# Norm statistics held by tokens, one number each, and spread over the features by TensorE

## What is computed

```python
def rms_norm(x, g):                       # mix0, ctx, ffn0, mix1, ffn1, fin, mix2, mlp2
    y = x * lax.rsqrt(jnp.mean(x * x, axis=-1, keepdims=True) + EPS)
    return y * g

def gated_deltanet(qkv, z, ...):          # 8 heads of 128
    q, k, v = jnp.split(jax.nn.silu(causal_depthwise_conv(qkv, conv_w)), 3, axis=-1)
    q, k = l2norm(q), l2norm(k)           # x * rsqrt(sum(x * x) + EPS), by head
    o = chunk_gated_delta_rule(q, k, v, g, beta)
    o = rmsnorm(o, out_norm) * jax.nn.silu(z)

def nsa_mixer(q, ..., k_s, ..., k_w, ...):   # heads of 64
    q = rmsnorm(q, q_norm) * (d ** -0.5)     # and rmsnorm of k_s and k_w
```

## Time and profile before

| what | value |
|---|---|
| median of 3 runs | 1294.68 us (1292.54 to 1296.09) |
| the profiled execution: its own time | 1292.29 us |
| its span, first to last instruction | 1290.5 us |
| mean clock granted to TensorE, share of full speed | 0.948 |
| PE busy | 1157.9 us, 90% of the span, 9,918 records |
| PEld busy | 1090.2 us, 84% |
| DVE busy | 899.5 us, 70% |
| ACT busy | 603.6 us, 47% |
| DVE `RECIPROCAL` on 128x512, 10 of them | 33.5 us |
| DVE `RECIPROCAL` on 128x256, 8 of them | 14.1 us |

### The profile page before, as it was taken

One profiled execution on the slowest core, in us unless ns is written; L12 is line 12 of the kernel. 1 busy time (PEld: TensorE's weight loads), 2 busy tenths in 40 slices (PEclk: granted clock), 3 DMA queues, 4 the chain that ended last, 5 costly groups with the idle time before them and its releaser, 6 DMA issues.

```text
span 1290.5 us, 23296 instructions
## 1 busy us (share of the span) xinstructions
PE 1157.9 (90%) x9918; PEld 1090.2 (84%) x9918; DVE 899.5 (70%) x1561; ACT 603.6 (47%) x1085; POOL 55.3 (4%) x70
## 2 busy tenths in 40 slices
PE   5878589999987999997988788778999999799999
PEld 1776479999987999996988676667998999799999
DVE  4956858988886666545668687878864975777443
ACT  2435535445445444543544556574323455555432
POOL 0000010000011000001000000001420001000000
PEclk9989789999998999999788898989999999899999
DMA  9741638888872575531344222112211555755520
GB/s 390 305 189 45 241 142 324 336 341 334 309 312 88 194 281 222 197 107 66 106 163 158 99 82 81 67 66 76 90 35 67 196 189 171 266 195 195 202 79 13
DMA packets 32360, 226.35 MB, mean 175 GB/s; under 512 B 3584, under 2 KB 4736, under 8 KB 5120
## 3 DMA queue, kind: packets, MB, share of 16 engines
q1 hardware_dynamic: 30528, 221.20, 46.3%
q10 hardware_dynamic: 1728, 3.67, 0.8%
HBM read 223.80 MB, written 1.05 MB: 174 GB/s over the span
## 4 chain that ended last, share of the span: by engine, by line
PE 63%; DVE 24%; ACT 9%; DMA 2%; issue 2%; POOL 0%; SPq 0%; DVEq 0%; ACTq 0%; POOLq 0%
PE bank L525 19%; PE bank L527 18%; PE bank L526 18%; DVE sb_wlo L1641 5%; ACT sb_whi L1175 2%; ACT sb_ss L1431 2%; DVE sb_nv L1908 2%; DVE sb_ring L1674 1%; DMA sb_ring<-in_ada 1%; DVE sb_ss L2025 1%; DVE sb_tmp L1660 1%; DVE sb_ss L2042 1%; DVE sb_rs L1652 1%; DVE sb_sq L2126 1%; DVE sb_Msb L2241 1%
## 5 line engine op out<-in xcount | busy, mean ns | idle before, releaser
L525 PE MATMUL bank<-sb_xh,sb_whi 128*128 128x256 f32 x1544 | 448.0, 290 | 28.8 <-DVE sb_xl L1665 12.1
L526 PE MATMUL bank<-sb_xl,sb_whi 128*128 128x256 f32 x1544 | 437.9, 284 | 0.0
L527 PE MATMUL bank<-sb_xh,sb_wlo 128*128 128x256 f32 x1544 | 437.6, 283 | 0.0
L525 PEld LDWEIGHTS bank<-sb_xh,sb_whi 128*128 128x128 f32 x1544 | 298.8, 194 | 41.3 <-issue 16.3
L1641 DVE TENSOR_TENSOR sb_wlo<-sb_ring,sb_whi 128x1024 fp32r<-128x1024 f32 (+1 forms) x201 | 243.8, 1220 | 126.1 <-ACT sb_whi L1175 125.6
L526 PEld LDWEIGHTS bank<-sb_xl,sb_whi 128*128 128x128 f32 x1544 | 301.2, 195 | 0.4 <-issue 0.2
L527 PEld LDWEIGHTS bank<-sb_xh,sb_wlo 128*128 128x128 f32 x1544 | 299.3, 194 | 0.0
L1175 ACT ACTIVATE sb_whi<-sb_ring 128x1024 fp32r<-128x1024 f32 (+1 forms) x201 | 210.8, 1052 | 93.6 <-PE bank L527 84.5
L1641 DVE TENSOR_TENSOR sb_wlo<-sb_more,sb_whi 128x1024 fp32r<-128x1024 f32 x108 | 131.3, 1223 | 71.5 <-ACT sb_whi L1175 71.1
L525 PE MATMUL bank<-sb_hh,sb_whi 128*128 128x256 f32 x608 | 172.1, 283 | 0.0
L527 PE MATMUL bank<-sb_hh,sb_wlo 128*128 128x256 f32 x608 | 172.1, 283 | 0.0
(11 more groups left out here) (338 smaller groups left out, 1773.8 us busy)
## 6 DMA issues: line engine op xcount, KB each, us to landing
sb_more<-in_w SPq DMA_DIRECT2D x34, 1024.0 KB, 6.2
sb_ring<-in_w SPq DMA_DIRECT2D x32, 1024.0 KB, 6.3
sb_ring<-in_adaT SPq DMA_DIRECT2D x26, 1024.0 KB, 7.9
sb_ring<-in_f SPq DMA_DIRECT2D x24, 1024.0 KB, 5.0
sb_more<-in_adaT SPq DMA_DIRECT2D x18, 1024.0 KB, 8.8
...
```

What stands on the lines that cost most here:

```text
L525: te.matmul(out, wh, rh, start=start, stop=False, skip_group_check=skip)
L526: te.matmul(out, wh, rl, start=False, stop=False, skip_group_check=skip)
L527: return te.matmul(out, wl, rh, start=False, stop=stop, skip_group_check=skip)
```

## The change

**Statistics by tokens.** The squares become the weights and one column of the ones the moving operand, so a matmul gives [128 tokens, 1]. Two of them (`t` = 0, 1) replace one of 256 columns. ACT takes the root out of PSUM on 128x2 with the mean and epsilon folded in (`deviation`), DVE the reciprocal on 128x2 (`inverse_deviation`), and a new function on PE, `spread`, brings it to all partitions: its weights are the column of reciprocals repeated 128 times by a step of zero, its moving operand the identity, its result a PSUM bank that `apply` reads. The new tile `dev` holds the numbers; `rs`, `rsx`, `nv` and `v8` are gone.

**The same in f1** (`heads2`, `hdev`, `f1_inverse`, `f1_spread`): four matmuls of two columns for two of 256, root and reciprocal on 128x8, then eight matmuls of 64 by 128 per pair, issued one unit later; the products L1914 move one unit later too.

**f2.** The order of the units becomes keys, queries, values (`F2`). Queries and keys are no longer scaled. The sums stay by tokens in `ksum` and `qsum`; `kroot` is the root of `ksum`, `beta` is multiplied by 1/`ksum`, the values are scaled by `kroot` as they are copied, and the queries' sums go into the output norm. Logarithm, exponentials and the eight scaling products are gone.

**Output norm.** The sums are four matmuls of one column per pair of heads, corrected with `qsum` in one small operation; root and reciprocal are on 128x16; 16 matmuls (`odb`) spread them before the products.

```diff
             def mean_square_rest(norm):
-                ps = take(RA, ("ms", norm), (dve, ("var", norm)))
+                ps = take(RA, ("ms", norm, 0), (act, ("sd", norm)))
...
-                te.matmul(ps[:, 0:T], ones, sq[:, 0, :], start=True, stop=False)
-                P.wait_ge(*act.at("sq", norm, KT - 1))
-                te.matmul(ps[:, 0:T], ones, sq[:, KT - 1, :], start=False, stop=True).then_inc(*pe.up(("ms", norm)))
+                for t in range(2):
+                    q = slice(t * 128, (t + 1) * 128)
+                    te.matmul(ps[:, t:t + 1], sq[:, 0, q], ones[:, 0:1], start=True, stop=False)
+                    P.wait_ge(*act.at("sq", norm, KT - 1))
+                    end = te.matmul(ps[:, t:t + 1], sq[:, KT - 1, q], ones[:, 0:1], start=False, stop=True)
+                end.then_inc(*pe.up(("ms", norm)))
+
+            def spread(norm):
+                ps = take(RO, ("spread", norm), (dve, ("used", norm)))
+                P.wait_ge(*dve.at("rs", norm))
+                for t in range(2):
+                    end = te.matmul(ps[:, t * 128:(t + 1) * 128], columns(dev[:, NORMS.index(norm), t:t + 1]), ident, start=True, stop=True)
+                end.then_inc(*pe.up(("spread", norm)))
...
             def f1_squares(j):
...
-                    end = te.matmul(ps[:, e * T:(e + 1) * T], blk, sq[:, (j - 1 + e) % 4, :], start=True, stop=True)
+                    end = column_sums(lambda t: hs[:, t, 2 * e:2 * e + 2], sq[:, (j - 1 + e) % 4, :], 0, heads2)
...
+            def f1_spread(j):
+                ps = take(RA, ("hb", j), (dve, ("nq", j)))
+                P.wait_ge(*dve.at("hrs", j))
+                for e in range(2):
+                    for t in range(2):
+                        o = e * T + t * 128
+                        for u, p in enumerate(HALVES):
+                            c = 2 * e + u
+                            end = te.matmul(ps[p, o:o + 128], columns(hdev[:, j // 2 % 2, t, c:c + 1], 64), ident, start=True, stop=True)
...
             pe.note("delta")
-            fill(7)
+            fill()
+            for p2 in range(4):
+                fill((1, 1, 2, 2)[p2])
+                ps = take(RA, ("odb", p2), (dve, ("on2", p2)))
+                P.wait_ge(*dve.at("odrs"))
+                for e in range(2):
+                    for t in range(2):
+                        o = e * T + t * 128
+                        end = te.matmul(ps[:, o:o + 128], columns(odev[:, t, 2 * p2 + e:2 * p2 + e + 1]), ident, start=True, stop=True)
...
-            def deviation(norm, r):
-                A.wait_ge(*dve.at("var", norm))
-                sc.activation(r[:, :], r[:, :], ACT.Sqrt).then_inc(*act.up(("sd", norm)))
+            def deviation(norm):
+                d = dev[:, NORMS.index(norm), :]
+                A.wait_ge(*pe.at("ms", norm))
...
+                    sc.activation(d, ps_of(("ms", norm, 0))[:, 0:2], ACT.Sqrt, bias=C("eps"), scale=1.0 / D).then_inc(*act.up(("sd", norm)))
...
+                if s == 11:
+                    A.wait_ge(*dve.at("qkv", 15))
+                    sc.activation(kroot[:, :, :], ksum[:, :, :], ACT.Sqrt, scale=0.25).then_inc(*act.up("kroot"))
...
             def unit_rms(j):
-                v2 = flat(nv[:, 0, (j % 4) - 1:(j % 4) + 1, :])
-                V.wait_ge(*act.at("hsd", j))
-                ve.reciprocal(v2, v2).then_inc(*dve.up())
...
+                V.wait_ge(*pe.at("hb", j))
...
             def f2_later(s):
-                for j0 in (7, 15):
...
-                        V.wait_ge(*act.at("len", j0, part))
-                        V.wait_ge(*dve.at("conv", j0))
-                        ve.tensor_tensor(q4, q4, v4, ALU.mult).then_inc(*dve.up(("len", j0, part)))
...
-                    ve.tensor_scalar(flat(v8[:, m - 1:m + 1, :]), ps_of(("qks", j))[:, :], 4 * EPS, None, ALU.add).then_inc(*dve.up(("qkv", j)))
```

More of the change, by code:

```diff
@@ L295 @@
 STEPS2 = [(j + 1) * (N2 + 1) // 24 - j * (N2 + 1) // 24 for j in range(24)]
+F2 = (*range(8, 16), *range(8), *range(16, 24))
 CUTS = ((0, 128), (128, 384))
+NORMS = ("mix0", "ctx", "ffn0", "mix1", "ffn1", "fin", "mix2", "mlp2")
 HALVES = (slice(0, 64), slice(64, 128))
@@ L538, in product, with column_sums @@
                 return end
+            def column_sums(out, src, c, ones_):
+                for t in range(2):
+                    end = te.matmul(out(t), src[:, c + t * 128:c + (t + 1) * 128], ones_, start=True, stop=True)
+                return end
             def mean_square(norm, k):
                 if k == 0:
-                    take(RA, ("ms", norm), (dve, ("var", norm)))
+                    for t in range(2):
+                        take(RA, ("ms", norm, t), (act, ("sd", norm)))
                 P.wait_ge(*act.at("sq", norm, k))
-                end = te.matmul(ps_of(("ms", norm))[:, 0:T], ones, sq[:, k, :], start=k == 0, stop=k == KT - 1)
+                for t in range(2):
+                    end = te.matmul(ps_of(("ms", norm, t))[:, t:t + 1], sq[:, k, t * 128:(t + 1) * 128], ones[:, 0:1], start=k == 0, stop=k == KT - 1)
                 if k == KT - 1:
@@ L582, in tensor_program @@
                 mean_square("ctx", k)
+            spread("mix0")
             def rotate(n):
@@ L600, in tensor_program @@
                     F.used(F.raw("adaT0"))
+                if n == 1:
+                    spread("ctx")
             rotate(3)
@@ L702, in tensor_program @@
             pe.note("layer0")
+            spread("ffn0")
             def swiglu(layer, norm, after):
@@ L739, in swiglu @@
                 pe.note(("hid", layer))
+                spread(after)
             swiglu(0, "ffn0", "mix1")
@@ L772, in tensor_program @@
             mean_square_rest("ffn1")
+            spread("ffn1")
             swiglu(1, "ffn1", "fin")
@@ L776, in tensor_program @@
                 mean_square("mix2", k)
+            spread("mix2")
             u, _ = F.take("tm0")
@@ L806, in f1 @@
                     f1_squares(j - 1)
+                if j < 12 and j % 2 and j > 1:
+                    f1_spread(j - 2)
             def hidden(e):
@@ L939, in tensor_program @@
             compressed2(1)
+            f1_spread(11)
             pe.note("f1")
@@ L962, in f2_later @@
                         P.wait_ge(*act.at("qksq", j - 1 + e))
-                        end = te.matmul(ps[:, e * T:(e + 1) * T], ones, sq[:, j % 8 - 1 + e, :], start=True, stop=True)
+                        end = column_sums(lambda t: ps[:, 2 * t + e:2 * t + e + 1], sq[:, j % 8 - 1 + e, :], 0, ones[:, 0:1])
                     end.then_inc(*pe.up(("qks", j)))
-                if 16 <= j < 24:
+                if j >= 16:
                     P.wait_ge(*dve.at("conv", j))
@@ L973, in tensor_program @@
             step = 2
-            for j in range(24):
-                if STEPS2[j]:
+            for s, j in enumerate(F2):
+                if STEPS2[s]:
                     attn_head(step)
@@ L1117, in tensor_program @@
                 end.then_inc(*pe.up(("od", p2)))
-                ps = take(RA, ("odss", p2), (dve, ("odvar", p2)))
+                if p2 == 0:
+                    sums = take(RO, "odss", (dve, "odvar"))[:, 0:16].rearrange("p (t n) -> p t n", t=2)
                 P.wait_ge(*act.at("odsq", p2))
-                te.matmul(ps[:, :], ones, sq3[:, p2 % 3, :], start=True, stop=True).then_inc(*pe.up(("odss", p2)))
+                for e in range(2):
+                    hd = 2 * p2 + e
+                    end = column_sums(lambda t: sums[:, t, hd:hd + 1], sq3[:, p2 % 3, :], e * T, ones[:, 0:1])
+                end.then_inc(*pe.up(("odss", p2)))
             pe.note("delta")
-            fill(7)
+            fill()
[3 more added lines that the diff above has]
+                P.wait_ge(*dve.at("odrs"))
+                for e in range(2):
+                    for t in range(2):
+                        o = e * T + t * 128
+                        end = te.matmul(ps[:, o:o + 128], columns(odev[:, t, 2 * p2 + e:2 * p2 + e + 1]), ident, start=True, stop=True)
+                end.then_inc(*pe.up(("odb", p2)))
             for j in range(8):
@@ L1132, in tensor_program @@
             pe.note("block2")
+            spread("mlp2")
             F.past(len(PLAN))
@@ L1190, in square @@
                 sc.activation(sq[:, k, :], src[:, k, :], ACT.Square).then_inc(*act.up(("sq", norm, k)))
-            def deviation(norm, r):
-                A.wait_ge(*dve.at("var", norm))
-                sc.activation(r[:, :], r[:, :], ACT.Sqrt).then_inc(*act.up(("sd", norm)))
+            def deviation(norm):
+                d = dev[:, NORMS.index(norm), :]
+                A.wait_ge(*pe.at("ms", norm))
+                if norm in ("mix0", "ctx", "mix2"):
+                    for t in range(2):
+                        sc.activation(d[:, t:t + 1], ps_of(("ms", norm, t))[:, t:t + 1], ACT.Sqrt, bias=C("eps"), scale=1.0 / D).then_inc(*act.up(*[("sd", norm)] * t))
+                else:
```

(1 more changed line is left out.)

219 lines of the change are left out of this document (115 added, 104 removed).

## The result

| | median of the runs, us | profiled execution's span |
|---|---|---|
| before | 1293.61 | 1290.5 |
| changed | 1276.84 (1271.31 to 1277.76) | 1275.7 |

A forecast was written before the change was run, and what follows sets the result against it. PE was taken as busiest (90% of the span, 63% of the chain), then DVE. Norms 10.5, f1 12, f2 12.5, less 0.8 for the output norm, make 34.2 off 1292.3: 1258 us, range 1241 to 1277.

The forecast's parts named there:

- So PE is done at 650.4 + 48 + 5.6 + 3 = 707: f1: start, PE's work at full clock, added spreads and idle time left, in us; PE done at 707 instead of 714.
- The last rival: f1 and norms: spreads wait for a reciprocal behind a DVE split; no chain shortened, within 4 us of 1292; chance 0.03.
- my 12: f1: 12 us gained, between 5 and 20, with DVE freed 13 us early and PE 7 early.
- Norms: the term: The eight norms: shorter chains and small reciprocals gain 10.5 us together, between 6 and 14.
- 0.107 per record: PE: price in us of a small matmul record with 128x128 weights, two records per matmul on 32-bit numbers.
- the clock's danger in a rival: f1 and f2, chiefly f2: small matmuls leave PE little to do, the clock drops, 1318 us; chance 0.05.
- The row with 64 columns: Profile row for PE: eight records with 64 moving columns in 1.00 us, giving the price of about 0.107 each.
- the second rival: All stages: full weight loads per one-column matmul, double for repeated weights; 17 us gained, 1275; chance 0.18.
- 12.5: f2: 12.5 us gained from DVE's relief and fewer stops for the logarithm, between 8 and 17.
- DVE's relief of 9.2: f2: DVE loses scaling products and copies, gains small operations, 9.2 us less; counted as 7.2 at busy share 0.8.
- The stops: f2: DVE's two stops of 3.71 us for the logarithm; one goes, one shortens, 5.4 us gained.
- 0.8 was forecast: Output norm: 0.8 us lost, between 2 won and 2 lost; added spreads cost 3.4, PE's gaps and shorter sums return part.

The follow-up runs named there:

- inv_only: The changed kernel with only f1's small reciprocal on DVE moved ahead of the split of the next unit's weights; 1271.4 us, ratio 0.9837.
- inv_slot5: The changed kernel with that reciprocal moved ahead and a fifth slot for the weight stream, sums still of one column; 1264.2 us, ratio 0.9764.

## Why the prediction was wrong in size

**f1: the step that failed.** "So PE is done at 650.4 + 48 + 5.6 + 3 = 707" left 3 us of waits for PE. In the 65 us printed above it is idle for 10.3, 10.0 of that ahead of the spreads; its busy time, 54.7, is near the 53.6 that I gave it, at a clock of 0.89. The prediction's own sign of being wrong, PE idle ahead of a spread by over 1 us, came with 5.9. I had counted what each engine has to do and not what a new hand-over waits behind. The last rival names that very thing, a spread waiting for a reciprocal that itself waits behind a split, and got a chance of 0.03. I even priced it, at one split per pair. What I hadn't seen is that the split in turn waits for a transfer, so that one of the stops is 5.9 us and not 1.2. The order of the rows of DVE in f1, printed above, shows the split ahead of the reciprocal. With the reciprocal in front, f1 gives 7.5 (inv_only), 10.5 with the slot too (inv_slot5), and 11 with wide sums besides: my 12 was near what the stage can give, not what this order gives.

**Norms: the term was mis-signed at the start.** mix0, ctx and ffn0 were to give 4.0 us. They cost 2.3 (204.8 before, a mean of 207.0 with one column), and with wide sums give 2.3 (202.5). The sums were costed as "0.107 per record", which was nearly right (0.112), and as free of consequence for the clock, which was wrong. I had the clock's danger in a rival, but in f2 and for want of work; it came at the start, with PE busy all the time. fin and mix2, 2.6 forecast, gave 0.2 to 1.0 and with wide sums 2.7 to 4.3. mix1 and ffn1, 2.6 forecast, gave 2.2 in one execution and nothing in the other, and mlp2 0 and 0.9. At ffn0 `spread` runs at the falling clock, so that chain saved 0.7 instead of 1.3.

**Small records.** The row with 64 columns was the right one to go by: 0.119 with tail. By the Trainium skill, "TensorE: Matmul & The Clock Gate", section "Back-to-back issue gap", a one-column matmul costs some 25 ns; the section says that its formula leaves the load of weights out, and in the trace, where weights of 128 columns go with each, the records stand 0.112 us apart, over four times that. The same page, section "LDWEIGHTS (loading the stationary operand)", has a load take the number of its columns over 1.2 in ns, 107 for 128, and at full clock the trace comes within 5% of that. f1's spreads took 1.09 for 16 where the clock was up, about the 0.058 of the earlier trace rows and a tail, and those of the output norm, which have 128 columns of repeated weights, start 0.111 apart. So the second rival's double price for repeated weights falls. Its 1275 lies 2 us from the time by luck: it had norms 7, f1 5, f2 8 and output norm -3, and the changed kernel's traces have 0.8 won or 2.2 lost, 0.5 to 1.5 lost, 16.5 and -2.6.

**f2: under-sized.** 16.5 where I had 12.5, inside its range of 8 to 17. I took DVE's relief of 9.2 times its busy share of 0.8 (which is 7.4, not the 7.2 written); it came in full, 8.6 less busy in that stretch. The stops were to give 5.4 and gave 6.9, since DVE had other work while ACT loaded its tables. The remaining 0.9 is less waiting elsewhere. These come from DVE's own busy and idle time in the traces; no run undoes f2 alone.

**Output norm: mis-sized.** 2.6 to 3.2 lost where 0.8 was forecast. The spreads stand 0.111 apart, 3.6 for the 32 where 3.4 was given, so of the 1.8 and 0.8 that were to come back at most 1.0 did.

**The rest.** In the two traces of the changed kernel my four terms come to 13.1 and 11.2 of the 34.2: norms 0.8 won and 2.2 lost, f1 1.5 and 0.5 lost, f2 16.4 and 16.5 won, output norm 2.6 lost in both. At the last split the traces are 14.6 and 11.8 ahead. Between the two stand 2.8 lost from 198 to 210 and from 228 to 246, and 4.3 and 3.4 won in products without an edit, which the sum had at nothing. The change of split 198 to 210, 1.8 slower in the changed kernel and 0.8 to 1.5 with the norms alone, has no cause that I can show.
